# Rotary embedding by GpSimd products and adding DMAs in place of TensorE products, with a new order around them

## The reference

```
proj = rmsnorm(h) @ w_in     # hq hf hi hgo hz | nq kcm vcm ksl vsl kwn vwn ngate nz
o_hg = rmsnorm(gated recurrence over tokens of hq, hf, hi) * sigmoid(hgo) * silu(hz)
qn   = rmsnorm(heads(nq)) * g;  q_rope = partial_rope(qn)
kc   = rmsnorm(compress(kcm));  vc = compress(vcm)   # 15 blocks of 32 tokens, MLP of 128
k_sl, k_wn = partial_rope(rmsnorm(heads(ksl))), partial_rope(rmsnorm(heads(kwn)))
o_nsa = g0 * attn(qn, kc, vc) + g1 * attn(q_rope, k_sl, v_sl) + g2 * attn(q_rope, k_wn, v_wn)
h = h + concat(o_hg, o_nsa * silu(nz)) @ w_out;   h = h + gate * (p @ w_pp)

def partial_rope(x, cos, sin):          # 16 of the 64 numbers of a head turn
    x1, x2, xp = x[..., :8], x[..., 8:16], x[..., 16:]
    return concatenate([x1 * c - x2 * s, x1 * s + x2 * c, xp], axis=-1)
```

## Time and profile before

| | |
|---|---|
| time, median of 3 runs | 989.2 us (988.89 to 989.45) |
| time of the profiled execution | 991.16 us |
| its span, first to last instruction | 989.5 us |
| TensorE busy | 968.3 us (98%) |
| VectorE busy | 754.5 us (76%) |
| ScalarE busy | 617.7 us (62%) |
| GpSimd busy | 6.9 us |
| granted TensorE clock | 1.0 over the whole span |

### The profile page before, as it was taken

How to read it: one execution, slowest core, us unless ns; L and a number is a source line. 1 busy time by engine, 2 the same in 40 slices (tenths; PEclk the granted TensorE clock), 3 DMA queues, 4 the chain that set the end, 5 groups by cost and what they waited for, 6 DMA issues and landing times.

```text
span 989.5 us, 18815 instructions
## 1 busy us (share of the span) xinstructions
PE 968.3 (98%) x7642; PEld 880.5 (89%) x7642; DVE 754.5 (76%) x1132; ACT 617.7 (62%) x918; POOL 6.9 (1%) x17
## 2 busy tenths in 40 slices
PE   6999999999999999999999999999999999999997
PEld 6998888998978889989998999999988988888886
DVE  7968676787676786797778776868977698768675
ACT  5745785676437775778467655556666576555564
POOL 2000000000000000000000000000000000000000
PEclk9999999999999999999999999999999999999999
DMA  9665513365637131835655656556473456655541
GB/s 304 200 167 171 171 60 112 123 218 172 174 118 229 44 124 53 272 117 182 202 170 174 210 172 202 178 187 203 120 235 99 148 168 198 191 195 184 178 161 43
DMA packets 143357, 164.00 MB, mean 166 GB/s; under 512 B 6302, under 2 KB 129832, under 8 KB 143288
## 3 DMA queue, kind: packets, MB, share of 16 engines
q1 hardware_dynamic: 142408, 161.97, 51.1%
q10 hardware_dynamic: 464, 0.93, 0.3%
q0 software_dynamic: 416, 0.12, 0.1%
HBM read 161.95 MB, written 1.05 MB: 165 GB/s over the span
## 4 chain that ended last, share of the span: by engine, by line
PE 79%; DVE 10%; ACT 4%; DMA 3%; issue 2%; SPq 0%; DVEq 0%; ACTq 0%
PE ps L483 16%; PE ps L484 16%; PE ps L485 16%; PE ps L1263 14%; PE ps L1261 7%; DVE panels_low L2005 3%; DMA panels<-in_w_in 2%; ACT panels_high L1377 2%; DVE squares L1968 1%; PE ps L501 1%; PE ps L688 1%; DVE input_parts L1964 1%; PE ps L713 1%; DMA panels<-in_w_pg 1%; PE ps L784 1%
## 5 line engine op out<-in xcount | busy, mean ns | idle before, releaser
L2005 DVE TENSOR_TENSOR panels_low<-panels,panels_high 128x2048 fp32r<-128x2048 f32 (+1 forms) x145 | 327.5, 2262 | 80.0 <-ACT panels_high L1377 79.8
L1377 ACT CAST panels_high<-panels 128x2048 fp32r<-128x2048 f32 (+1 forms) x145 | 273.1, 1886 | 101.4 <-PE ps L485 64.0
L483 PE MATMUL ps<-input_parts,panels_low 128*128 128x256 f32 x832 | 241.6, 290 | 2.2 <-DVE panels_low L2005 1.5
L484 PE MATMUL ps<-input_parts,panels_high 128*128 128x256 f32 x832 | 235.2, 283 | 0.0
L485 PE MATMUL ps<-input_parts,panels_high 128*128 128x256 f32 x832 | 235.1, 283 | 0.0
L1263 PE MATMUL ps<-input_parts,panels_high 128*128 128x512 f32 x608 | 214.0, 395 | 0.0
L1261 PE MATMUL ps<-input_parts,panels_low 128*128 128x256 f32 x608 | 170.6, 281 | 0.7 <-DVE panels_low L2005 0.7
L483 PEld LDWEIGHTS ps<-input_parts,panels_low 128*128 128x128 f32 x832 | 159.1, 191 | 7.4 <-issue 3.9
L484 PEld LDWEIGHTS ps<-input_parts,panels_high 128*128 128x128 f32 x832 | 159.2, 191 | 0.7 <-issue 0.5
L485 PEld LDWEIGHTS ps<-input_parts,panels_high 128*128 128x128 f32 x832 | 159.2, 191 | 0.0
L1263 PEld LDWEIGHTS ps<-input_parts,panels_high 128*128 128x128 f32 x608 | 114.1, 188 | 26.4
(11 more groups left out here) (342 smaller groups left out, 1620.8 us busy)
## 6 DMA issues: line engine op xcount, KB each, us to landing
panels<-in_ffn_up SPq DMA_DIRECT2D x44, 1024.0 KB, 5.1
panels<-in_w_in SPq DMA_DIRECT2D x29, 1024.0 KB, 5.5
panels<-in_ffn_down SPq DMA_DIRECT2D x22, 1024.0 KB, 4.8
panels<-in_mix_w_in SPq DMA_DIRECT2D x20, 1024.0 KB, 5.5
panels<-in_w_out SPq DMA_DIRECT2D x8, 1024.0 KB, 5.0
panels<-in_w_pg SPq DMA_DIRECT2D x8, 1024.0 KB, 5.1
panels<-in_mix_w_out SPq DMA_DIRECT2D x8, 1024.0 KB, 5.2
panels<-in_w_in SPq DMA_DIRECT2D x6, 512.0 KB, 5.7
```

The costliest lines, as they stand in the source:

```text
L483: pe.matmul(dst, w[1], x[0], start=start, stop=False if not kw else True, **kw)
L484: pe.matmul(dst, w[0], x[1], start=False, stop=False if not kw else True, **kw)
L1377: nc.scalar.copy(high_slots[slot][:, 0:size], raw[n % SLOTS][:, 0:size]).then_inc(high_ready, 1)
L2005: V.tensor_tensor(low_slots[slot][:, 0:size], raw[n % SLOTS][:, 0:size], high_slots[slot][:, 0:size].bitcast(F32), ALU.subtract).then_inc( ...
```

## The change

1. The products with identity and `rot` go (four per layer for queries, two for keys), with `rot` itself and ScalarE's two copies to `QR`. GpSimd multiplies `QN` by the cosine table straight into `QR` and by the sine table into `UW`; then four DMAs from its queue, of 8 partitions each, add the sine rows to `QR` on the partner rows (`accum_op=ALU.add`; the sign now sits in the sine table). The same for the keys into `UK`. VectorE's four products per layer go. The scores wait for the DMAs (`q_turned`) and for the padded keys (`kz_ready`).
2. `hid4` moves ahead of the value projection.
3. Both sums and level 6 come ahead of the entries `q_norm` and `k_norm`; `hid` follows, then a gate chunk, level 7 and another chunk.
4. `k_pad` moves behind `o_square`, waits for the keys' DMAs and reads SBUF; `o_norm` waits for it.
5. ScalarE casts up to hgo1 behind the key factor, VectorE makes its low part between the query norm and the key norm, and on both engines splits are let in again after `hidden` (before: ScalarE after the copy of qr1, VectorE after `cmp_kv`).

```diff
@@ const_table
-    rot = np.zeros((P, P))
...
-        sin[h:h + 8] = np.sin(ang.astype(np.float32))
+        sin[h:h + 8] = np.sin(ang.astype(np.float32)) * (-1 if h % 64 else 1)
@@ TensorE
+                (the block of hid4, with its releases and todo(("hidden_parts",)), from below)
                 tokens([f"vv{n}_{l}" for n in range(NT)], 5, [(f"vv{h}", l) for h in range(2)], VV,
                        lambda: some(2))
                 todo(("gates",))
                 pe.wait_ge(qsq_ready, l + 1)
                 for j in range(2):
                     product(f"qss{j}_{l}", 1 + j, 512, head_ones, SQ[:, j * 512:(j + 1) * 512])
-                todo(("q_norm",))
                 pe.wait_ge(ksq_ready, l + 1)
                 product(f"kss_{l}", 4, 512, head_ones, UK[:, 0:512])
-                todo(("k_norm",))
                 some(2)
-                (the block of hid4, then gate_chunk())
+                todo(("q_norm",))
+                todo(("k_norm",))
                 drained(pe, f"hid4_{l}")
...
                 todo(("hidden",))
-                pe.wait_ge(rope_ready, l + 1)
-                for j in range(2):
-                    begin(f"qr{j}_{l}", 1 + j)
-                    pe.matmul(ps[1 + j][:, :], ident, UW[:, j * 512:(j + 1) * 512], start=True, stop=False)
-                    done(f"qr{j}_{l}", pe.matmul(ps[1 + j][:, :], const("rot"),
-                                                 UW[:, 1024 + j * 512:1024 + (j + 1) * 512],
-                                                 start=False, stop=True))
-                    todo(("copy", f"qr{j}"))
+                gate_chunk()
                 some(2)
                 gate_chunk()
-                (the same for the keys: wait, kr, two products, todo(("k_pad",)))
                 pe.wait_ge(w2_landed, 48 * (l + 1))
                 pe.wait_ge(hidden_ready, l + 1)
...
                 todo(("o_square",))
+                todo(("k_pad",))
                 gate_chunk()
...
-                drained(pe, f"qr1_{l}")
-                drained(pe, f"kr_{l}")
+                pe.wait_ge(q_turned, 64 * (l + 1))
+                pe.wait_ge(kz_ready, l + 1)
@@ ScalarE
                     elif step == "k_norm":
                         head_rinv([f"kss_{l}"], UK[:, 512:1024], 64, 512).then_inc(k_rinv_ready, 1)
+                        split_high(place, SPLIT_NO[("hgo1", l)] + 1)
...
-                        src = v3(bank(name), 2)
+                        act.wait_ge(k_turned, 64 * (l + 1))
+                        src = UK[:, 0:512].rearrange("p (k t) -> p k t", k=2)
...
-                        act.wait_ge(rope_ready, l + 1)
+                        act.wait_ge(kz_ready, l + 1)
...
-                    parts_out = (parts_out or step == "hidden_parts") and (step, *arg) != ("copy", "qr1")
+                    parts_out = (parts_out or step == "hidden_parts") and step != "hidden"
@@ VectorE
                     elif kind == "q_norm":
                         dve.wait_ge(q_rinv_ready, l + 1)
-                        (norm of QN, then QN x cos and QN x sin into UW)
+                        V.scalar_tensor_tensor(QN[:, :], QN[:, :], GQ[:, l:l + 1], HZ[:, :],
+                                               ALU.mult, ALU.mult).then_inc(q_normed, 1)
+                        split_low(place, SPLIT_NO[("hgo1", l)] + 1)
                     elif kind == "k_norm":
-                        (two norms of KN, then KN x cos and KN x sin into UK)
+                        (two norms of KN, the second with .then_inc(k_normed, 1))
...
-                    parts_out = (parts_out or kind == "hidden_parts") and kind != "cmp_kv"
+                    parts_out = (parts_out or kind == "hidden_parts") and kind != "hidden"
@@ GpSimd
+            def turned(terms, cosine, table, heads):
+                return nc.gpsimd.tensor_tensor(cosine.rearrange("p (j t) -> p j t", j=heads),
+                                               terms.rearrange("p (j t) -> p j t", j=heads),
+                                               const(table).unsqueeze(1).to_broadcast([P, heads, T]), ALU.mult)
+
+            half_rows = [(h + a, h + 8 - a) for h in (0, 64) for a in (0, 8)]
+            pool.wait_ge(const_landed, 16)
+            for l in range(DEPTH):
+                pool.wait_ge(q_normed, l + 1)
+                turned(QN[:, :], QR[:, :], "cos", 4)
+                turned(QN[:, :], UW[:, 1024:2048], "sin", 4).then_inc(rope_ready, 1)
+                pool.wait_ge(rope_ready, l + 1)
+                for src, dst in half_rows:
+                    pool.dma_start(QR[dst:dst + 8, :], UW[src:src + 8, 1024:2048], accum_op=ALU.add).then_inc(q_turned, 16)
+                pool.wait_ge(k_normed, l + 1)
+                turned(KN[:, :], UK[:, 0:512], "cos", 2)
+                turned(KN[:, :], UK[:, 512:1024], "sin", 2).then_inc(k_rope_ready, 1)
+                pool.wait_ge(k_rope_ready, l + 1)
+                for src, dst in half_rows:
+                    pool.dma_start(UK[dst:dst + 8, 0:512], UK[src:src + 8, 512:1024], accum_op=ALU.add).then_inc(k_turned, 16)
```

More of the change, by code:

```diff
@@ L372, in build @@
         kc_rinv_ready, o_rinv_ready = sem("cmp_k_rinv_ready"), sem("hg_o_rinv_ready")
+        q_normed, k_normed = sem("q_normed"), sem("k_normed")
         rope_ready, k_rope_ready = sem("q_rope_terms_ready"), sem("k_rope_terms_ready")
+        q_turned, k_turned = sem("q_sine_terms_added"), sem("k_sine_terms_added")
+        kz_ready = sem("k_padded_ready")
         blocks_ready = sem("cmp_blocks_ready")
@@ L819, in _ @@
                     todo(step)
[L820 to L824, removed]
-                for j in range(2):
-                    product(f"qss{j}_{l}", 1 + j, 512, head_ones, SQ[:, j * 512:(j + 1) * 512])
-                todo(("q_norm",))
-                pe.wait_ge(ksq_ready, l + 1)
-                product(f"kss_{l}", 4, 512, head_ones, UK[:, 0:512])
-                todo(("k_norm",))
-                some(2)
                 pe.wait_ge(blocks_ready, l + 1)
@@ L845, in _ @@
                 todo(("hidden_parts",))
-                gate_chunk()
+                tokens([f"vv{n}_{l}" for n in range(NT)], 5, [(f"vv{h}", l) for h in range(2)], VV,
+                       lambda: some(2))
+                todo(("gates",))
+                pe.wait_ge(qsq_ready, l + 1)
+                for j in range(2):
+                    product(f"qss{j}_{l}", 1 + j, 512, head_ones, SQ[:, j * 512:(j + 1) * 512])
+                pe.wait_ge(ksq_ready, l + 1)
+                product(f"kss_{l}", 4, 512, head_ones, UK[:, 0:512])
+                some(2)
+                todo(("q_norm",))
+                todo(("k_norm",))
                 drained(pe, f"hid4_{l}")
@@ L1563, in _ @@
                 log_exp()
-                dest = {"nq0": QN[:, 0:512], "nq1": QN[:, 512:1024], "qr0": QR[:, 0:512], "qr1": QR[:, 512:1024],
-                        "ct": PCT[:, :], "hgo0": SG[:, 0:512], "hgo1": SG[:, 512:1024],
+                dest = {"nq0": QN[:, 0:512], "nq1": QN[:, 512:1024], "ct": PCT[:, :], "hgo0": SG[:, 0:512], "hgo1": SG[:, 512:1024],
                         "hz0": HZ[:, 0:512], "hz1": HZ[:, 512:1024], "nz0": NZ[:, 0:512], "nz1": NZ[:, 512:1024]}
@@ L1615, in _ @@
                     elif step == "k_pad":
-                        name = f"kr_{l}"
-                        full(act, name)
-                        src = v3(bank(name), 2)
+                        act.wait_ge(k_turned, 64 * (l + 1))
+                        src = UK[:, 0:512].rearrange("p (k t) -> p k t", k=2)
                         for g in range(2):
@@ L1623, in _ @@
                             ins = nc.scalar.copy(kz[64:128, :, 1, g, :], s)
-                        ins.then_inc(free(name), 1)
+                        ins.then_inc(kz_ready, 1)
                     elif step == "spread":
@@ L2326, in _ @@
                             s = slice(j * T, (j + 1) * T)
[L2327 to L2334, removed]
+                            ins = V.scalar_tensor_tensor(KN[:, s], KN[:, s], vec("nsa_knorm_g", 3 * l + 1 + j),
+                                                         UK[:, 512 + j * T:512 + (j + 1) * T], ALU.mult, ALU.mult)
+                        ins.then_inc(k_normed, 1)
                     elif kind == "hidden":
```

7 lines of the change are left out of this document (removed).

## The result

The changed kernel takes 1000.88 us (median of four runs, 1000.05 to 1001.77) where the kernel before takes 989.33: 1.0117 of its time, with a 95% interval of 1.0100 to 1.0135. That is 11.6 us slower. I had predicted 984, with a range of 979 to 995. The profiled execution took 1001.1 us and has a span of 999.1.

A forecast was written before the change was run, and what follows sets the result against it. TensorE, busy for 98% of the span, was taken to bound the kernel. From 989.2 us, 8.4 came off for earlier cross products and 3.5 was added for GpSimd holding VectorE up: 984.3, put down as 984, range 979 to 995.

The forecast's parts named there:

- the ceiling: Level 4 to cross product, both layers: 12.0 us gain if TensorE's removed products and layer 1's extra waiting came off whole.
- VectorE's chain: VectorE's work from level 6 through level 7 in layer 0, ending at 100.7; it keeps 3.6 us of the possible gain.
- The low part of hgo1: VectorE, between query norm and key norms: takes 2.28 us, 2.2 from start to start, ending at 94.3.
- The signs that I named against myself: Among them: low parts or key norms 2 us longer during GpSimd's products; level 4 to cross product above 30 us.
- The first rival: Between query norm and level 7, VectorE waits for all GpSimd products, 6.8 us per layer: 994.4 us; chance 0.36.
- The hold-up d: Time GpSimd's products hold VectorE up, delaying the cross product: 1.75 us per layer, 3.5 in both.
- My upper bound, 6.8: Most that GpSimd's products could hold VectorE up per layer: two query products at 2.28 us, two key products at half.
- The cross product starts at 100.8: TensorE, layer 0: starts right after VectorE's level 7 (100.7), instead of at 104.35.
- the whole forecast gain of 3.55: Layer 0: cross product 3.55 us earlier, at 100.8 instead of 104.35, before any hold-up by GpSimd.
- TensorE waiting about 1 us twice: Layer 0: waits for hidden values (wanted 95.6, there 96.5) and before the cross product (wanted 100.1, starts 100.8).
- I predicted 27.66 us: TensorE from level 4 to the cross product: about 27.7 us in both layers, against 29.46 in layer 0 before.
- The adding DMAs: GpSimd's queue: four issues take 2 us, landing 5.3, without cost; the rival that they come late, 1027 us, had chance 0.05.

The follow-up runs named there:

- e6: Changed kernel with VectorE making the four rotary products behind level 7, hidden sums ahead of level 6, hgo1 in bank 1; 978.91 us, ratio 0.9899 to the kernel before.
- e1: Changed kernel with GpSimd's four products per layer cut to eight columns, order, waits and DMAs kept; 988.58 us, ratio 0.9995.
- e2: Changed kernel with the hgo1 projection in PSUM bank 1 instead of bank 0, nothing left out; 991.94 us, ratio 1.0033.
- e7: Changed kernel with VectorE's chain reordered so that GpSimd's four products fall behind level 7; 997.84 us, ratio 1.0087.
- e5: Changed kernel with nine unused fp32 filler products of 512 columns per layer in TensorE's idle time; 1000.33 us, ratio 1.0126.
- e4: Kernel before with only the rotary step changed (GpSimd products, adding DMAs, padding behind o_square), old order otherwise; 996.17 us, ratio 1.0076.

## Why the prediction was wrong

**What held.** The loss and every part of it lie between level 4 and the cross product, in both layers alike. TensorE was spared what I counted: e6's stretches give the ceiling. VectorE's chain was right too: without hold-up I had it through level 7 at 100.7, 25.8 us behind level 4; e1 has it through at 100.06, 25.4 us behind. The low part of hgo1 took 2.28 us, as forecast. The signs that I named against myself are there: key norms longer by 4.2 us, a stretch above 30. The first rival's mechanism came true, but its 994.4 us were 6.5 too few.

**The hold-up d, mis-sized: the first step that failed.** I took 1.75 us per layer, the middle between none and VectorE's own 3.5, from a row that says nothing of GpSimd. In the changed kernel the key norms take 4.20 us more (5.08 for 0.88) and level 7's two products 1.87 more (1.21 and 1.48 for 0.41 each): d = 6.07. My upper bound, 6.8, was made the right way (two products as long as a low part, two at half); GpSimd's took 2.51 alone where I had 2.28. The choice inside the range was wrong. The rule of the Trainium skill that I weighed (SBUF — State Buffer, Who interferes with whom) says just this: the later one waits for the whole of the other. The runs agree, in both directions: a low part at 4.49 us for 2.28 in e2, a product of GpSimd at 4.29 for 2.51 in the changed kernel. In e7 GpSimd's wait, 5.4 us, is longer than any one of VectorE's instructions there, which is more than the rule says. Of the durations, a query product took 2.51 us by itself; from the Trainium skill's figure, which is for an addition (GPSIMD Engine Reference, Performance versus the Vector engine), it would be 2.25, half of 4497 ns, as an estimate.

**A wait that I left out: the second.** "The cross product starts at 100.8", right behind level 7, supposed that hgo1's chunk had run by then. Its first product opens bank 0, which level 7's second half holds until VectorE's copy. So the cross product comes a chunk (2.95 us at full clock) after that copy. In e1, without hold-up, this and the clock are the 4.0 us between the end of level 7 and the cross product, of which the clock has 1.5 (4.47 less 2.97): more than the whole forecast gain of 3.55. e2, which changes only the bank, shows the other side: 4.4 us less in layer 0, what this wait and the lower clock behind it cost together.

**The clock: the third, which had no term.** I had TensorE waiting about 1 us twice. In e6, which hardly waits, the clock is 1.00 throughout; here, after 4.8 idle us, TensorE had half of it, and the chunk took 4.97 us for 2.97 with fillers (e5): 2.0 us per layer.

Summed for layer 0: I predicted 27.66 us. To this add 3.9 for d (level 7 ends 31.45 us after level 4 where I had 27.56), 2.5 for the chunk behind the copy (2.95 and 0.15 for the key sum, less the 0.6 by which it starts before level 7's end), 2.0 for the clock: 36.1, measured 35.95; the 0.1 is what I had put between the end of level 7 and the cross product. With d alone set right my own sum would have given 989.2 - 8.4 + 12.1 = 992.9 us, inside the range. So d alone doesn't explain the miss: the other two terms, 4.5 us per layer and 9.0 in both, stood nowhere in the sum; with them it is 1001.9, and 1000.88 was measured.

**What was right at no cost.** The adding DMAs: four take GpSimd 3.3 us to issue and each lands about 3 us after, where I had 2 and 5.3; the two errors nearly cancel. No wait follows from them in the changed kernel; the padding starts at 119.63 right behind ScalarE's squares of `o`. The chance of 0.05 for them was fair.

## What to carry to other kernels

An engine that is idle is no free engine: here the work moved to GpSimd cost VectorE about its full length where VectorE read from SBUF meanwhile, so cost it at one after the other, in both directions, and put it where neither is wanted. Before work is said to run ahead, ask of each piece which bank it opens and who empties that bank. And a wait of some 5 us on TensorE costs more than itself: here 2 us more, at the clock behind it. What a filler wins there is not all found in the time (2.4 of 4 us). In this kernel VectorE's order by what TensorE asks for next, with the products on VectorE behind it and one bank changed, made 22 us between two kernels that do the same work on TensorE.

## What the runs showed of the hardware that I had not expected

- The order of two starts 0.05 to 0.25 us apart sets who pays: in e2, layer 1, the compressed key product waited 8.15 us, in layer 0 4.79, with the same program.
- GpSimd can be kept out for 5.4 us by VectorE instructions that follow each other closely, though none of them is longer than 2.28 us (7.88 less 2.51, e7).
- A VectorE copy from SBUF to SBUF with one input took 3.22 us for 0.23 (e2): by the rows it began 0.65 us ahead of GpSimd's first key product (304.44) and ended with it (306.85). A `TENSOR_SCALAR` took 1.25 for 0.18 (e4); two copies out of PSUM kept their 0.57.
- A gate panel's DMA of 1 MB landed after 5.0 us in most places and after 7.2 to 7.7 in a few; in e5, where it took 7.3, the last 2.5 us moved 23 to 27 GB/s.
- Even eight columns cost GpSimd 0.42 us a product (e1: the second one alone).
- Idle time is paid for at the clock behind it, not in it: hgo1's chunk began at 105.99, ran without a break, and still had 0.51 until 110.6, then 1.00.
